# Five transformer layers on one core: two norms as one weighted sum, and another order at the second norms

## What is computed

```python
def rmsnorm(x, g):
    return x * lax.rsqrt(jnp.mean(x * x, axis=-1, keepdims=True) + 1e-6) * g

# each layer, in both models:
h = rmsnorm(x, norm1) * (1 + scale1) + shift1
x = x + gate1 * mixer(h)
h = rmsnorm(x, norm2) * (1 + scale2) + shift2
x = x + gate2 * feed_forward(h)
# between the two models:
x = rmsnorm(x, final_norm)
```

## Time and profile before

| what | value |
|---|---|
| runs | 1607.1 us median of 3 (1606.55 to 1608.4) |
| the profiled execution | 1608.79 us, of which 1607.0 us are the span on the core |
| granted PE clock, mean | 0.991 |
| PE busy | 1543.6 us, 96% |
| DVE busy | 1196.5 us, 74% |
| ACT busy | 784.8 us, 49% |
| POOL busy | 89.2 us, 6% |
| HBM read | 381.62 MB, 240 GB/s over the span |
| issue to landing of a weight unit, median | 6.3 us |
| issue to landing of a bias load, median | 3.3 us |

### The profile page before, as it was taken

How to read it: one execution, slowest core, us unless ns; L and a number is a source line. 1 busy time by engine, 2 the same in 40 slices (tenths; PEclk the granted TensorE clock), 3 DMA queues, 4 the chain that set the end, 5 groups by cost and what they waited for, 6 DMA issues and landing times.

```text
span 1607.0 us, 30721 instructions
## 1 busy us (share of the span) xinstructions
PE 1543.6 (96%) x12474; PEld 1471.9 (92%) x12474; DVE 1196.5 (74%) x1721; ACT 784.8 (49%) x1029; POOL 89.2 (6%) x95
## 2 busy tenths in 40 slices
PE   2979999999999999999999999999999999999998
PEld 1858999999999999998899999889999898899998
DVE  6898877788578777865587777968777778676665
ACT  2454433356464333565443335564333567664543
POOL 0150000000000000011000000210000013200000
PEclk8999999999999999999999999999999999999999
DMA  9855887846258878563488785347888455345550
GB/s 390 352 186 209 356 323 289 312 186 235 80 210 336 324 287 333 211 235 132 158 349 324 287 321 186 142 158 302 330 309 315 181 184 170 123 159 183 177 183 26
DMA packets 54331, 383.77 MB, mean 239 GB/s; under 512 B 6356, under 2 KB 6612, under 8 KB 8560
## 3 DMA queue, kind: packets, MB, share of 16 engines
q1 hardware_dynamic: 50400, 363.75, 60.2%
q0 software_dynamic: 3856, 18.97, 3.4%
HBM read 381.62 MB, written 4.22 MB: 240 GB/s over the span
## 4 chain that ended last, share of the span: by engine, by line
PE 83%; DVE 11%; DMA 3%; ACT 2%; issue 1%; POOL 0%; SPq 0%; DVEq 0%; ACTq 0%
PE PS L1875 70%; DVE wlo L1326 4%; PE PS L1896 3%; DMA CST<-cst_in 1%; PE PS L1945 1%; DVE adar L1344 1%; DMA adar<-ada 1%; PE PS L2069 1%; PE PS L2019 1%; ACT whi L918 1%; DVE SCR L1498 1%; PE PS L2046 1%; DMA raw<-ada 1%; PE PS L1919 1%; PE PS L1909 1%
## 5 line engine op out<-in xcount | busy, mean ns | idle before, releaser
L1875 PE MATMUL PS<-hhi,whi 128*128 128x256 f32 x2496 | 713.5, 286 | 2.7 <-DVE wlo L1326 2.6
L1326 DVE TENSOR_TENSOR wlo<-raw,whi 128x2048 fp32r<-128x2048 f32 x234 | 537.1, 2297 | 237.1 <-ACT whi L918 236.6
L1875 PE MATMUL PS<-hlo,whi 128*128 128x256 f32 x2496 | 707.3, 283 | 0.0
L1875 PE MATMUL PS<-hhi,wlo 128*128 128x256 f32 x2496 | 707.3, 283 | 0.0
L918 ACT ACTIVATE whi<-raw 128x2048 fp32r<-128x2048 f32 x234 | 447.0, 1912 | 480.9 <-PE PS L1875 467.1
L1875 PEld LDWEIGHTS PS<-hhi,whi 128*128 128x128 f32 x2496 | 479.8, 192 | 9.7 <-issue 7.6
L1875 PEld LDWEIGHTS PS<-hlo,whi 128*128 128x128 f32 x2496 | 480.1, 192 | 1.3 <-issue 1.2
L1875 PEld LDWEIGHTS PS<-hhi,wlo 128*128 128x128 f32 x2496 | 480.0, 192 | 0.0
L1344 DVE CUSTOM_DVE_ANT_0 adar<-adar,CB 128x1024 f32<-128x1024 f32 x232 | 277.9, 1238 | 10.6 <-DMA adar<-ada 10.4
L1875 PE MATMUL PS<-ahi,whi 128*128 128x256 f32 x968 | 274.5, 284 | 1.1 <-DVE alo L1825 1.1
L1875 PE MATMUL PS<-alo,whi 128*128 128x256 f32 x968 | 273.9, 283 | 0.0
(11 more groups left out here) (226 smaller groups left out, 1299.0 us busy)
## 6 DMA issues: line engine op xcount, KB each, us to landing
raw<-weights SPq DMA_DIRECT2D x234, 1024.0 KB, 6.3
adar<-ada SPq DMA_DIRECT2D x104, 1024.0 KB, 5.9
adar<-ada POOLq DMA_DIRECT2D x12, 1024.0 KB, 5.4
raw<-ada SPq DMA_DIRECT2D x4, 1024.0 KB, 15.2
bias_rows<-bias_of_distance POOLq DMA_DIRECT2D x1, 3072.0 KB, 16.6
adar<-bias_rows POOLq DMA_DIRECT2D x8, 256.0 KB, 3.3
CST<-cst_in SPq DMA_DIRECT2D x1, 1128.0 KB, 22.7
CB<-c_in SPq DMA_DIRECT2D x2, 512.0 KB, 4.1
```

Source lines behind the costliest of these rows:

```text
L1326: v.tensor_tensor(wlo[:, u % CV, :], raw[:, u % RAW, :], whi[:, u % CV, :].bitcast(F32), ALU.subtract).then_inc(lo_done, 1)
L1875: m = pe.matmul(o, w(a), h(b), start=first and k_ == 0, stop=last and k_ == 2, skip_group_check=True)
```

## The change

Three things change.

1. The two norms ahead of layer 5 become one. In the prologue FW = sqrt(final gain squared + EPS) is formed for each feature. The squares ahead of layer 5 are those of FW * X, each block by itself; their mean plus EPS squared, inverse root, is the product of the final norm's root and that of layer 5's first norm. AFF is multiplied by the final gain, and XN comes from X as it is. The DVE scaling of X (L1390) and the second sum are gone.
2. X itself is scaled later, in the mixer of layer 5: ACT squares it once more (four instructions), DVE adds these (1024, 512 and 256 columns), PE sums one block within unit 2, ACT forms the root into XR, and POOL multiplies the eight blocks by XR and then by the gain, sixteen instructions behind the bias loads of pairs 0 and 1 and ahead of that of pair 2. DVE's ada sums there move behind the low half of unit 3. The first update of X by an output unit waits for the last of POOL's.
3. At all five second norms block 6 is updated first, then come the two additions, then the low half's first 1024 columns, block 7, and the other 1024 columns. PE starts the pair of units when the first part is there and waits for the second ahead of block 4.

```diff
@@ -890,6 +894,12 @@
                     bias_load(1)
+                    pool.wait_ge(x_root, 1)
+                    for k in range(C):
+                        pool.tensor_tensor(X[:, k, :], X[:, k, :], XR, ALU.mult).then_inc(x_rooted, 1)
+                    for k in range(C):
+                        pool.wait_ge(x_rooted, k + 1)
+                        pool.tensor_scalar(X[:, k, :], X[:, k, :], par("gain", 1, 8 * plan.final_norm + k), None, ALU.mult).then_inc(x_ready, 1)
                     for p in range(2, PAIRS):
...
@@ -932,6 +942,11 @@
                     act.wait_ge(x_ready, 8 * (n - 1) + k + w)
+                if n == plan.final_norm:
+                    for c in range(k, k + w):
+                        e = act.activation(XN[:, c, :], X[:, c, :], ACT.Square, scale=FW[:, c:c + 1])
+                    e.then_inc(norm_sq, 1)
+                    return
                 act.activation(XN[:, k:k + w, :], X[:, k:k + w, :], ACT.Square).then_inc(norm_sq, 1)
...
@@ -939,11 +954,22 @@
                 act.wait_ge(norm_sum, n + 1)
-                root(RB[:, 0, :], RB[:, 1, :], bank[3][:, 0:S], D).then_inc(norm_r, 1)
+                root(RB[:, 0, :], RB[:, 1, :], bank[3][:, 0:S], D, eps2 if n == plan.final_norm else epsb).then_inc(norm_r, 1)
+
+            def final_squares(n):
+
+                act.wait_ge(norm_lo, C * (plan.split_norm(n) + 1))
+                for k in range(0, C, 2):
+                    act.activation(XN[:, k:k + 2, :], X[:, k:k + 2, :], ACT.Square).then_inc(norm_sq, 1 if k < C - 2 else 2)
+
+            def final_root(n):
+
+                act.wait_ge(norm_sum, n + 1)
+                root(XR_LOG, XR, bank[6][:, 0:S], D).then_inc(x_root, 1)
...
-                if n:
+                if n and plan.place[n] != "scaled":
                     norm_roots(n)
...
@@ -955,6 +981,9 @@
             if has_b2:
+                act.wait_ge(final_w, 1)
+                link(act.activation(FW, FW, ACT.Ln, bias=epsb[:]))
+                act.activation(FW, FW, ACT.Exp, scale=0.5)
...
@@ -1181,12 +1210,14 @@
                     hi(u0 + 2)
+                    final_squares(plan.norm[l])
                     square_read(0)
...
                     hi(u0 + 4)
+                    final_root(plan.norm[l])
                     triple_read(2)
...
@@ -1325,6 +1356,13 @@
+            def lo_part(u, part):
+
+                v.wait_ge(hi_done, u + 1)
+                half = slice(UNIT // 2 * part, UNIT // 2 * part + UNIT // 2)
+                e = v.tensor_tensor(wlo[:, u % CV, half], raw[:, u % RAW, half], whi[:, u % CV, half].bitcast(F32), ALU.subtract)
+                e.then_inc(lo_done if part else lo_first, 1)
+
...
@@ -1364,6 +1402,18 @@
                 v.wait_ge(aff_s, 2 * l + which + 1)
+                if kinds[l] == "b2" and which == 0:
+                    link(v.tensor_tensor(AFF[:, 0, :], AFF[:, 0, :], par("gain", 8, 8 * plan.final_norm), ALU.mult))
+
+            def final_adds(n):
+
+                for k, after in ((4, 5 * n + 5), (2, None), (1, None)):
+                    if after:
+                        v.wait_ge(norm_sq, after)
+                    else:
+                        v.wait_ge(norm_add, added[0])
+                    added[0] += 1
+                    v.tensor_tensor(XN[:, 0:k, :], XN[:, 0:k, :], XN[:, k:2 * k, :], ALU.add).then_inc(norm_add, 1)
...
@@ -1379,29 +1429,27 @@
-                v.wait_ge(norm_r, n + 1)
+                v.wait_ge(norm_r, n + (plan.final_norm is None or n < plan.final_norm))
...
                 for k in range(C):
-                    if l is None:
-                        v.scalar_tensor_tensor(out=X[:, k, :], in0=X[:, k, :], scalar=par("gain", 1, 8 * n + k), in1=RB[:, 1, :],
-                                               op0=ALU.mult, op1=ALU.mult).then_inc(x_ready, 1)
-                    else:
-                        v.scalar_tensor_tensor(out=XN[:, k, :], in0=X[:, k, :], scalar=AFF[:, which, k:k + 1], in1=RB[:, 1, :],
-                                               op0=ALU.mult, op1=ALU.mult).then_inc(norm_h, 1)
-                        if k >= 2:
-                            low(k - 2)
-                if l is not None:
-                    low(C - 2)
-                    low(C - 1)
+                    v.scalar_tensor_tensor(out=XN[:, k, :], in0=X[:, k, :], scalar=AFF[:, which, k:k + 1], in1=RB[:, 1, :],
+                                           op0=ALU.mult, op1=ALU.mult).then_inc(norm_h, 1)
+                    if k >= 2:
+                        low(k - 2)
+                low(C - 2)
+                low(C - 1)
             link(v.memset(zeros[:], 0.0))
+            v.memset(eps2[:], EPS * EPS)
...
             v.wait_ge(par_in_s, 16)
+            if has_b2:
+                v.tensor_tensor(FW, par("gain", C, 8 * plan.final_norm), par("gain", C, 8 * plan.final_norm), ALU.mult).then_inc(final_w, 1)
...
@@ -1428,8 +1476,6 @@
             for l, kind in enumerate(kinds):
-                if kind == "b2":
-                    norm(plan.final_norm)
                 if l == 0:
...
@@ -1707,8 +1753,9 @@
                     lo(u0 + 2)
+                    final_adds(plan.norm[l])
+                    lo(u0 + 3)
                     ada_all(mixer_ada(l)[0])
-                    lo(u0 + 3)
                     lo(u0 + 4)
...
@@ -1759,33 +1806,38 @@
-                for i in range(OUT_UNITS):
+                def x_add(i, t):
+
+                    k = 2 * i + t
+                    v.scalar_tensor_tensor(out=X[:, k, :], in0=out_bank(i, t), scalar=MOD[:, 48 * l + 16 + k:48 * l + 17 + k], in1=X[:, k, :],
+                                           op0=ALU.mult, op1=ALU.add).then_inc(x_ready, 1)
+
+                for i in range(OUT_UNITS - 1):
...
                         ada_read(9)
-                    if i == OUT_UNITS - 1:
-                        add_squares(plan.norm[l] + 1, 4, 5, 3)
-                        add_squares(plan.norm[l] + 1, 0, 4)
-                    else:
-                        v.wait_ge(pe_unit, plan.uout[l] + i + 1)
+                    v.wait_ge(pe_unit, plan.uout[l] + i + 1)
...
                         v.wait_ge(ada_mod, ADA_UNITS * l + 5 + 1)
-                    for t in range(2):
-                        k = 2 * i + t
-                        if i == OUT_UNITS - 1:
-                            if t == 0:
-                                v.wait_ge(out_half, l + 1)
-                            else:
-                                v.wait_ge(pe_unit, plan.uout[l] + i + 1)
-                        v.scalar_tensor_tensor(out=X[:, k, :], in0=out_bank(i, t), scalar=MOD[:, 48 * l + 16 + k:48 * l + 17 + k], in1=X[:, k, :],
-                                               op0=ALU.mult, op1=ALU.add).then_inc(x_ready, 1)
+                        if kind == "b2":
+                            v.wait_ge(x_ready, 8 * plan.norm[l])
+                    x_add(i, 0)
+                    x_add(i, 1)
...
                         add_squares(plan.norm[l] + 1, 0, 2)
+                v.wait_ge(out_half, l + 1)
+                x_add(OUT_UNITS - 1, 0)
+                add_squares(plan.norm[l] + 1, 4, 5, 3)
+                add_squares(plan.norm[l] + 1, 0, 4)
+                lo_part(plan.uffn[l] + 1, 0)
+                v.wait_ge(pe_unit, plan.uout[l] + OUT_UNITS)
+                x_add(OUT_UNITS - 1, 1)
+                lo_part(plan.uffn[l] + 1, 1)
...
@@ -1910,7 +1962,10 @@
                 unit_ready(u)
-                unit_ready(u + 1)
+                if first_low:
+                    pe.wait_ge(lo_first, first_low)
+                else:
+                    unit_ready(u + 1)
                 if high:
...
@@ -1960,9 +2017,7 @@
             for l, kind in enumerate(kinds):
-                if kind == "b2":
-                    sum_squares(plan.final_norm)
-                sum_squares(plan.norm[l])
+                sum_squares(plan.final_norm if kind == "b2" else plan.norm[l])
                 u0 = plan.uin[l]
...
@@ -2184,8 +2239,13 @@
+                def final_sum(n):
+
+                    pe.wait_ge(norm_add, adds_to(n) + 3)
+                    pe.matmul(bank[6][:, 0:S], ones, XN[:, 0, :], start=True, stop=True).then_inc(norm_sum, 1)
+
                 if kind == "b2":
-                    unit(2, lambda: (aux_product(0), aux_product(1)))
+                    unit(2, lambda: (aux_product(0), final_sum(plan.norm[l]), aux_product(1)))
                     unit(3)
```

18 lines of the change are left out of this document (12 added, 6 removed).

## The result

The changed kernel takes 1599.35 us (median of 5 runs, 1598.77 to 1599.70), the kernel before 1607.73 beside it (5 runs, 1606.55 to 1608.71): a ratio of 0.9941 (95% interval 0.9931 to 0.9951). The forecast was 1596.2 with a range of 1594.3 to 1600.3. The direction and the range held; of the 10.9 us of the sum 8.4 came.

A forecast was written before the change was run, and what follows sets the result against it. TensorE, busy 96% of the span, bounds the kernel; time comes only from standstills, halved clock or omitted products. 7.7 + 1.4 + 2.3 - 0.5 = 10.9 us off the 1607.1 median gave 1596.2, range 1594.3 to 1600.3.

The forecast's parts named there:

- (1): Ahead of layer 5: one sum gives both roots, saving 7.7 us, with ends 7.4 and 8.0.
- (2): Fifth mixer: scaling X there costs 0.5 us for TensorE's added sum; the other moved work costs nothing.
- +0.5 us on the path: Fifth mixer: TensorE's one more sum, two records, 0.43 us steady or 0.64 cold, taken as 0.5 us.
- the thin spot: Fifth mixer: head norms end at 1305.5, scores need them at 1306.1, 0.6 us of room; POOL's delay taken as 0.
- rival D: The fifth mixer gives back 1 to 4 us, by a head norm waiting for POOL or late low halves; chance 0.14.
- well over 0.7 us: Sign of being wrong: POOL's instructions on X in the fifth mixer take well over 0.7 us.
- Rival E: Slower: POOL's sixteen instructions hold the third bias load past the third mask, 6.6 us of room; 1607.1 + 3.2 and more; chance 0.03.
- (3): Second norms: 0.35 us less in each of four layers, 1.4 in all, and 2.3 us less in the first layer.
- up to 0.1: Second norms of layers 2 to 5: gain from block 7's sum no longer queueing behind block 6's, up to 0.1 us.
- B: First layer's clock stays down or falls behind block 7's wait, returning 1.2 to 1.5 us; 1597.5; chance 0.12.
- C: Second norms give nothing, as another link sets the start; 8.3 us gained, 1598.8; chance 0.08.
- (4): Prologue: a memset, one multiplication and two tiny exponent steps fall where engines wait for first loads; costs nothing.

The follow-up runs named there:

- a1: The kernel before with the new order of the second norms alone; 1603.14 us, ratio 0.9972.
- e1: The kernel before with twelve idle TensorE products between the two sums ahead of layer 5; 1608.0 us, ratio 0.9998.
- b1: The changed kernel with POOL's sixteen instructions on X put behind the bias load of pair 2; 1597.55 us, ratio 0.9932.
- b2: The changed kernel with the fifth mixer's ada sums back ahead of the low half of unit 3; 1598.28 us, ratio 0.9937.
- d1: The changed kernel with the low half whole and ahead of block 7 in the second norms; 1602.92 us, ratio 0.9962.
- a2: The changed kernel with the old order of the second norms, so one norm for two alone; 1601.91 us, ratio 0.9961.

## Why the prediction was right, and where not

**(1) One norm for two: right to 0.1 us in the profiles.** 7.7 was forecast, 12.78 - 5.19 = 7.59 came. Inside it the shares were different: the squares cost up to 0.4 us and not 0.2, since each takes 0.40 us and two take the place of one of 0.63, so that the sum waits; AFF's 0.2 us lie under the later root, so the two together still cost 0.48 (8.07 - 7.59), some 0.1 more than the forecast's 0.4. The halved stretch went, and nothing new took its place. What the term did not say is that 1.7 of its 7.7 us were a fall of the clock taken from one profile. I had put the sum against the median, with that piece as if every run had it. The profiled execution of before stood 1.1 us above the median of its five runs; that of the change stood on its median (1599.36). The difference of the two executions is 9.4 us, that of the medians 8.4, and this is where most of the gap between them can lie; a1 and e1 show the stretch at 11.1, and the runs of e1 lie no lower than those of before; but whether the fall is missing in most runs of before stays open.

**(2) The fifth mixer: the step that failed.** "+0.5 us on the path" for the sum was right: 0.43. The clock times of the chain were right too; moved by the 10.53 us between the two starts of this mixer, 1301.8, 1304.0 and 1305.5 for VectorE's steps become 1291.3, 1293.5 and 1295.0, and b1, without POOL beside it, shows the head norms done at 1295.0 on a clock 0.18 later. But at the thin spot, for which I "keep 0 to 0.6 us, and take 0", 0.98 us were lost: MOD, QT and KT were 0.55 + 0.57 + 0.47 us longer beside POOL, 1.6 us against 0.6 of room. I had bounded the delay by one POOL instruction of 0.6 us, though three VectorE instructions with both inputs in SBUF stood in that spot, each with its own. This is rival D at its lower end, 1 us. The move of the ada sums, which the forecast had made the room so thin by, was not needed: with them where they were (b2) the head norms are slowed too and nothing waits.

**POOL** was mis-sized, and this sign of being wrong, "well over 0.7 us", came: 0.61 us an instruction was taken for both forms. Undisturbed, in b1, the form with a broadcast operand takes 0.73; the shortest of the scalar form take 0.91. Beside VectorE the medians are 0.96 and 1.01, by all instructions of one tile in the changed kernel (shortest, median and longest ns):

```profile
L899 POOL TENSOR_TENSOR X<-X,acc x8: 717/961/2782, 1294.0 to 1301.8; 128x256 f32<-128x256 f32 x8
L902 POOL TENSOR_SCALAR X<-X,PAR x8: 912/1006/3386, 1304.6 to 1313.7; 128x256 f32<-128x256 f32 x8
```

20.8 us in all and an end at 1314.7 (1325.2 on the clock of before) where 1319 was forecast. Rival E had 6.6 us of room there and 6.2 of them were used; the third mask still did not wait for a bias, also because it stood 1.4 us later itself: VectorE idles 2.12 us ahead of it for TensorE, as before. The longest of the scalar form, 3.39 us, is the sixth; the first is not an outlier. The GPSIMD Engine Reference of the Trainium skill (Instruction dispatch) would have allowed about 6 us for a first call of a freshly loaded routine; no instruction of this work shows it.

**(3) Second norms: right.** 2.31 us in layer 1 against 2.3, and 0.30 against 0.35 in each other layer: block 7 came 0.28 us earlier as worked out, and the "up to 0.1" for an unqueued sum was 0.02. d1, with a whole low half ahead of block 7, bears the mechanism out (4.76 where 4.75 was expected). B did not occur in the profiles of the change. The halved clock in that stretch goes with the long wait: the four profiles that have TensorE idle for 1.92 to 2.21 us there (before, a2, d1, e1) show it, at 7.89 to 8.34 us, and the ten in which its longest wait is 0.85 do not, at 5.58 or 5.59. C is refuted by four equal 0.30.

**(4) Prologue: right as far as it shows.** The first product stands at 39.93 before and at 40.09 after; over all profiles it lies from 39.9 to 41.3, and the mixer of layer 1 behind it takes 99.7 to 101.4 with the clock, so the start can't tell tenths.

In all: 10.9 forecast; -0.1 in (1), -0.9 in (2), -0.2 in (3) make 9.7 in the stages. The medians give 8.4, another 1.3 less; the clock ahead of layer 5 could be that, but it isn't shown. Another 0.6 of the 3.15 us between forecast and result are the base, 1607.1 by three runs and 1607.73 by five. The forecast's own terms gave 9.7 to 11.9 us (11.9 only with the added sum at nothing; with its least, 0.43, some 11.5), and 8.4 lies below them: the range held by what the rivals B, C and D had added to it.

## What to carry to other kernels

When work is given to an idle engine, look at the tightest spot that it overlaps on the engine it shares a resource with, count every instruction there and give each its own delay; moving either the new work (b1) or the late work (b2) took the wait away and made no other. Read a gain stage by stage, between two records of the bounding engine, and keep a halved clock apart as a term with its own chance: it may be gone in the next run, or stand elsewhere. When an engine works without a pause up to the last link, an earlier input from elsewhere gains nothing.
